# Reading the moving operand of fp32r products from two halves of its 512 columns

## The reference

```python
def first_block(x, ...):
    for layer in range(2):
        h = rms_norm(x, norm_g[layer, 0]) * (1.0 + scale) + shift
        y = nsa_mixer(h, ...) if layer % 2 == 0 else hgrn2_mixer(h, ...)
        x = x + gate * y
        h = rms_norm(x, norm_g[layer, 1]) * (1.0 + scale) + shift
        x = x + gate * hier_moe(h, ...)     # 16 experts, top 2: (silu(x @ w1) * (x @ w3)) @ w2

def second_block(x, ...):
    for l in range(2):
        x = x + 0.5 * swiglu(rmsnorm(x, ffn1_norm[l]), gate, up, down)   # 1024 -> 2752 -> 1024
        h = rmsnorm(x, mix_norm[l])
        p_a, p_b, p_c = _split(h @ w_in[l], (A_IN, B_IN, C_IN))
        o_a, o_b, o_c = rwkv7_mixer(...), dsa_mixer(...), retention_mixer(...)
        x = x + concatenate([o_a, o_b, o_c]) @ w_out[l]
        x = x + 0.5 * swiglu(rmsnorm(x, ffn2_norm[l]), gate, up, down)
    return rmsnorm(x, final_norm)
```

## Time and profile before

| | us |
|---|---|
| three runs, median | 4058.69 |
| three runs, lowest and highest | 4055.40, 4058.89 |
| the profiled execution's own time | 4054.44 |
| its span, first to last instruction | 4052.6 |
| PE busy in the span | 3887.6 (96%) |
| DVE busy, ACT busy | 2531.8 (62%), 1961.2 (48%) |
| chain of work that ended last, on PE | 80% |

### The profile page before, as it was taken

How to read it: one execution, slowest core, us unless ns; L and a number is a source line. 1 busy time by engine, 2 the same in 40 slices (tenths; PEclk the granted TensorE clock), 3 DMA queues, 4 the chain that set the end, 5 groups by cost and what they waited for, 6 DMA issues and landing times.

```text
span 4052.6 us, 59941 instructions
## 1 busy us (share of the span) xinstructions
PE 3887.6 (96%) x25080; PEld 3073.2 (76%) x25080; DVE 2531.8 (62%) x4297; ACT 1961.2 (48%) x3260; POOL 240.5 (6%) x213
## 2 busy tenths in 40 slices
PE   7999999999989999989999989999999999899998
PEld 5855788877867888868878667888788887578886
DVE  4288589985275899954456855544544469655445
ACT  3366588884364888842234434322423344343222
POOL 0033100000021000010000000000000000000000
PEclk9999999999999999999999999999999999899999
DMA  5464399982202999932222101222222221012221
GB/s 234 185 231 186 139 426 416 415 338 104 86 21 87 402 418 414 370 121 104 94 87 90 38 24 45 102 88 94 94 104 104 85 98 47 3 43 104 86 101 68
DMA packets 62566, 637.83 MB, mean 157 GB/s; under 512 B 6567, under 2 KB 6823, under 8 KB 27480
## 3 DMA queue, kind: packets, MB, share of 16 engines
q1 hardware_dynamic: 47032, 578.42, 36.3%
q0 software_dynamic: 8640, 31.46, 2.1%
q10 hardware_dynamic: 6624, 24.12, 1.5%
HBM read 603.52 MB, written 35.69 MB: 158 GB/s over the span
## 4 chain that ended last, share of the span: by engine, by line
PE 80%; DVE 12%; ACT 5%; issue 2%; DMA 1%; POOL 0%; DVEq 0%; POOLq 0%; SPq 0%; ACTq 0%
PE ps L366 13%; PE ps L370 13%; PE ps L371 13%; PE ps L1567 4%; PE ps L1569 4%; PE ps L1568 4%; DVE wbuf_r L347 3%; PE ps L1589 2%; PE ps L1588 2%; PE ps L1587 2%; DVE arena L3332 1%; DVE arena L3330 1%; PE ps L622 1%; PE ps L415 1%; PE ps L416 1%
## 5 line engine op out<-in xcount | busy, mean ns | idle before, releaser
L370 PE MATMUL ps<-arena_r,wbuf_r 128*128 128x512 f32 x2688 | 1047.5, 390 | 0.0
L347 DVE TENSOR_TENSOR wbuf_r<-slot,wbuf_r 128x512 fp32r<-128x512 f32 (+2 forms) x824 | 587.0, 723 | 652.6 <-ACT wbuf_r L337 651.1
L337 ACT ACTIVATE wbuf_r<-slot 128x512 fp32r<-128x512 f32 (+2 forms) x824 | 498.9, 613 | 623.3 <-PE ps L371 532.2
L366 PE MATMUL ps<-hT_r,wbuf_r 128*128 128x512 f32 x2016 | 794.7, 394 | 5.4 <-DVE arena_r L771 4.4
L371 PE MATMUL ps<-hT_r,wbuf_r 128*128 128x512 f32 x2016 | 786.1, 390 | 0.0
L370 PEld LDWEIGHTS ps<-arena_r,wbuf_r 128*128 128x128 f32 x2688 | 505.7, 188 | 104.7 <-issue 2.6
L366 PEld LDWEIGHTS ps<-hT_r,wbuf_r 128*128 128x128 f32 x2016 | 379.3, 188 | 95.3 <-issue 5.8
L371 PEld LDWEIGHTS ps<-hT_r,wbuf_r 128*128 128x128 f32 x2016 | 379.3, 188 | 80.0
L366 PE MATMUL ps<-arena_r,wbuf_r 128*128 128x512 f32 x704 | 277.3, 394 | 0.9 <-DVE arena_r L2780 0.9
L371 PE MATMUL ps<-arena_r,wbuf_r 128*128 128x512 f32 x672 | 261.4, 389 | 0.0
L1435 DVE TENSOR_TENSOR arena_r<-arena,arena_r 128x1024 fp32r<-128x1024 f32 x164 | 195.9, 1220 | 45.6 <-ACT arena_r L1428 45.2
(11 more groups left out here) (582 smaller groups left out, 7011.8 us busy)
## 6 DMA issues: line engine op xcount, KB each, us to landing
arena<-in_moe SPq DMA_DIRECT2D x82, 2048.0 KB, 10.6
slot<-in_moe SPq DMA_DIRECT2D x56, 2048.0 KB, 10.4
slot<-in_gu SPq DMA_DIRECT2D x40, 2048.0 KB, 7.7
slot<-in_ada SPq DMA_DIRECT2D x20, 2048.0 KB, 8.0
slot<-in_down SPq DMA_DIRECT2D x16, 2048.0 KB, 7.8
slot<-in_win SPq DMA_DIRECT2D x12, 2048.0 KB, 7.7
yrow<-arena ACTq DMA_DIRECT2D x46, 512.0 KB, 10.8
slot<-in_hgrn SPq DMA_DIRECT2D x8, 2048.0 KB, 7.9
```

The costliest lines, as they stand in the source:

```text
L337: a.activation(hi[:, 0:w], src[:, off:off + w], ACT.Copy).then_inc(*act.mark(c.name, "hi", i))
L347: v.tensor_tensor(lo[:, 0:w], src[:, off:off + w], hi[:, 0:w].bitcast(F32), ALU.subtract) \
L366: p.matmul(bank, hi[:, cs], rh[:, k, :], start=k == 0, stop=False, skip_group_check=True)
L370: p.matmul(bank, hi[:, cs], rl[:, k, :], start=False, stop=False, skip_group_check=True)
```

## The change

A helper `by_halves` gives a view of 512 columns in which positions 0, 1, 2, 3 are columns 0, 256, 1, 257 and so on: the first dimension of the access steps by 256 columns and has two elements, the second steps by one column and has 256. The moving operand of the products named above is read through this view. For the result to stand in PSUM in its usual order, the data have to lie in SBUF with the even columns in the first half and the odd ones in the second:

- weights that move are laid out so by the host (`_halved`): the experts' weights, the columns for `tok3_pe` of width 512, the scan's span matrix;
- activation tiles that move are written through the same view, by ACT (hi) and DVE (lo, which also reads the hi tile through it): the input norms of the four feed-forward stages, the gated hidden tiles, and the split outputs of the mixers.

The input projections of the mixers stay as they were (`cols=in_order`), since their tokens also serve as stationary operand; so do `tok3_pe` of width 264 and all plain f32 products. No instruction, wait, transfer or buffer is added, removed or moved: on each engine the rows stand in the same order with the same waits, and differ only in the shape of an access (an ACT write of 128x512 is 128x256x2 after the change).

```diff
+def by_halves(x):
+    return x.rearrange("p (a b) -> p b a", a=2)
+
+def in_order(x):
+    return x
...
-                    p.matmul(bank, hi[:, cs], rh[:, k, :], start=k == 0, stop=False, skip_group_check=True)
+                    p.matmul(bank, hi[:, cs], cols(rh[:, k, :]), start=k == 0, stop=False, skip_group_check=True)
...
+                hi_cols, lo_cols = (by_halves(x) if width == 512 else x for x in (hi, lo))
...
-                    p.matmul(o, rh[:, k, cs], hi, start=k == 0, stop=False, skip_group_check=True)
+                    p.matmul(o, rh[:, k, cs], hi_cols, start=k == 0, stop=False, skip_group_check=True)
...
-            a.activation(m.gh[:, f, :], m.sg[f % 4], ACT.Copy).then_inc(*act.mark(n, "g hi", part, f))
+            a.activation(by_halves(m.gh[:, f, :]), m.sg[f % 4], ACT.Copy).then_inc(*act.mark(n, "g hi", part, f))
...
-                    v.tensor_tensor(m.gl[:, f, :], sg, m.gh[:, f, :].bitcast(F32), ALU.subtract) \
+                    v.tensor_tensor(by_halves(m.gl[:, f, :]), sg, by_halves(m.gh[:, f, :].bitcast(F32)), ALU.subtract) \
...
-                            p.matmul(bank, xh[:, ks], hi[:, cs], start=k == 0, stop=False, skip_group_check=True)
+                            p.matmul(bank, xh[:, ks], by_halves(hi[:, cs]), start=k == 0, stop=False, skip_group_check=True)
...
+def _halved(w):
+    return np.ascontiguousarray(w.reshape(*w.shape[:-1], -1, 256, 2).swapaxes(-1, -2)).reshape(w.shape)
...
-    out["moe"] = np.concatenate([m1, m3, m2], axis=1)
+    out["moe"] = _halved(np.concatenate([m1, m3, m2], axis=1))
```

More of the change, by code:

```diff
@@ L348, in cut_lo, with lin3_pe @@
                 .then_inc(*dve.mark(c.name, "lo", i))
[L350 removed]
+        def lin3_pe(p, c, ps, pieces, name, count, rh, rl, end, kt=8, ready=None, first=0, stacked=False, cols=by_halves):
             for i in range(first, first + count):
@@ L374, in lin3_pe, with two3_pe @@
                 pe.also(*name, i)
-        def two3_pe(p, c, ps, pieces, name, tiles, rh, rl, end, by, ready):
+        def two3_pe(p, c, ps, pieces, name, tiles, rh, rl, end, by, ready, cols=by_halves):
             bank = [ps.take((*name, i), end(i)) for i in tiles]
```

94 lines of the change are left out of this document (49 added, 45 removed).

## The result

The changed kernel took 3999.95 us (median of 4 runs, 3998.07 to 4007.14) beside 4057.05 us for the kernel before on the same chip: a ratio of 0.9868, 95% interval 0.9849 to 0.9887. By the medians it is 57 us faster (1.4%), by the ratio 1.3%. The forecast was 121 us.

The account below looks back on a forecast made before the run. PE was taken as the bound nearly everywhere; feed-forward 74 + experts 35 + `tok3_pe` 5 + outputs 7 = 121 us off 4054.4 gave 3933, or 3937 for a median, with a range of 3905 to 4066.

Parts of the forecast that it names:

- part (221): All altered products: only the overrun growing with columns goes, 5.7 ns each, 62 us in all, 3998 us; chance 0.20.
- nothing (227): All altered products: pace unchanged, the overrun lies elsewhere, writes cost 0 to 8 us, 4058 to 4066 us; chance 0.13.
- slower (428): All altered products: alternating fetch takes two ticks a column, 2190 us lost, near 6250 us or in between; chance 0.22.
- the f32 row: Eight f32 products in the earlier trace: 428 ns each, halved 214 for 512 columns, so the overrun lies in the operand fetch.
- the 74 forecast: Feed-forward stages: 6016 products x 12.2 ns give 73 us saved, plus 1 us from products in `two3_pe`.
- 26 for 35: Expert stages: 3312 products x 12.2 ns give 40 us, of which 35 were taken as saved.
- 5 us off for DMA: Expert stages: DMA falls 0.3 to 0.7 us behind a block, partly hidden by slack, so 35 of 40 us are taken.
- The forecast's own sign for the DMA: Expert stages: if ACT begins to wait for DMA, the 35 us saved were too many.
- 0 to 2: Alternate writes by ACT and DVE: 14 uncovered input norm tiles x 0.13 to 0.7 us, 2 to 10 us; 0 to 2 taken.
- The gated tiles have the 70 us as cover: Feed-forward stages: ACT waits 70 us for the gated tile before writing g hi, which hides slower gated writes.
- the line through both widths: Products of 264 and 512 columns: fit of 6.4 ns plus 0.430 ns a column, splitting the 13 ns overrun.
- L512, L2745 and L2800 within 0.13 us: Norm and gated tile writes in the feed-forward: times expected to stay within 0.13 us of 0.75, 0.63 and 0.69 us.

Follow-up runs that it names:

- reads: Changed kernel with every activation tile written in order, all altered products still reading by halves: 3952.87 us, ratio 0.9749 to the kernel before.
- outs: Kernel before with alternate writes only in the output tiles of attention, hgrn and the two mixers: 4072.72 us beside 4050.48, ratio 1.0055.
- writes: Kernel before with only the alternate activation writes, everywhere the change has them, products reading in order: 4104.62 us, ratio 1.012.
- patterns: Code of reads, with single 512-column products each read in its own order (pairs apart, steps, parts in turn): 216 to 460 ns a product, whole time 4557 us.

## Why the forecast was wrong

**The mechanism, right.** The pace of an altered product fell, the projections beside it stayed at 227, and every other rival fell with that: part (221), nothing (227), slower (428). Nothing but the order of the moving columns differs between 216 and 227 ns, so most of the overrun was in the fetch of the moving operand, as the f32 row had suggested.

**The size of one product, near.** 216 ns and not 214.5, so 10.7 ns saved and not 12.2. The Trainium skill's "TensorE: Matmul & The Clock Gate", section "Wait — 56ns, not 53.3ns?", had 215.7, and the trace agrees. The f32 records of the earlier trace rows start 429 ns apart in the median, 2.3 ns over their two ticks a column, and the new pace is 2.7 ns over one tick a column: half of an f32 record holds only half of what each record has of its own.

**The reads, 102 of 121.** By stages, kernel before against `reads`: feed-forward stretches 345.1 to 329.5 three times and 345.1 to 328.8 once, 63 us for the 74 forecast. Experts 12.9 and 13.2, 26 for 35. `tok3_pe` 1.1 + 3.4, 4.5 for 5. Outputs 2.3 + 1.1 + 4.4 + 1.9, 10 for 7. Together 103. Of the 18 missing, 11 are in the feed-forward, where the pace alone explains 9 (6016 x 1.5 ns), and 9 in the experts, where it explains 5, less 3 gained in the outputs. That gain is partly luck: 192 products 10.7 ns faster are 2 us, and the last output got 4.4, with a clock of 1.00 where the kernel before had 0.94.

**The experts, a discount too small and for a wrong reason.** 3312 products x 10.7 ns are 35 us, of which 26 came. The forecast took 5 us off for DMA, 9 were lost, and a reading of the profile could have gone on blaming the DMA: landings grew from 10.6 to 15.8 us, the engines' DMA share stayed at 1.01, and 7.34 MB at 427 GB/s are 17.2 us, exactly a block. But half the fetch changed nothing. The forecast's own sign for the DMA, ACT waiting for it, did not appear either. The 92.5 us of DVE in 100 stood in the forecast beside it, "become 97%", and no price was put on them; a piece that DVE finishes 0.46 us late once a block was what ended last.

**The step that failed: the writes.** The forecast took "0 to 2" us and put 10 at the far end; measured 50. Two faults stand in that line. First the price. It was taken from a DVE row with one operand every 64 bytes, 31 columns, 259 ns against 251, and in that row it is a source that is read so; a scattered destination stood nowhere in the trace. The measured price, 0.43 to 0.49 us a tile, lies between the forecast's two ends (0.13 and 0.7). Thirty-one columns in 251 ns, beside 512 in 693, cannot show a price for each column well either. Second, and heavier, the count. It asked which altered tile PE waits for, and found 14. With the measured price these give 6 to 7 us, so the price alone does not explain 50. Three things were left out. The 32 output tiles were not counted at all: PE waits for 13 of them in `outs`, which took 22 us more. The untouched cuts of the weights stand in the same queues behind the norm tiles: PE's waits for them grew by 13 us in `writes`. And the granted clock stood lower: by the estimate above 17 us of the 50, 12 of them already in the 22. "The gated tiles have the 70 us as cover" held for most of them, but not for the last one of a stage: PE waited 4.3 us for it in the four stages, where it had waited 0.9.

**Small slips in the working.** A block of 72 x 226.7 + 12 x 112 ns is 17.7 us and not 17.8. Of the 13 ns over one tick a column the line through both widths gives 6.9 to the columns and 6.4 to the product; the text has them the other way round, and its rival takes 5.7 because it sets out from 214.5 and not from 213.3. The range's lower end, 3905, is some 9 us below 4058.7 - 145. None of this changes the outcome.

**What would have told.** The forecast said what would show the writes wrong, L512, L2745 and L2800 within 0.13 us; their rows in the changed kernel did, 0.4 to 0.5 us longer. The range, 3905 to 4066, held the time. It was the likeliest value that was 63 us off. That the time, 3999.95, meets the 3998 of the rival "only part of the overrun goes" is chance: that rival wanted products 221 ns apart and next to no cost in the writes, and neither came.

**The rule on lines.** Beside the rival of 6250 us stood the Trainium skill's "SBUF — State Buffer", table of specifications, which wants at least two accesses to a line of 16 bytes for full bandwidth. As a forecast for alternate reads it was wrong: one access in a row to each line ran fastest of all, 216 ns. The price that the rival had, two ticks a column, exists, 451 ns for a step of 2, though that step does touch each line twice in a row. That a line is fetched anew, as the third theory of `patterns` had it, and every price here are not in that table. For writes the rule agrees with the rows: two and two 674 ns, one and one 1142. The measurement decides: for TensorE's reads the rule sorts the table above if it is taken for every other read, and not for reads as they follow each other.

## What to carry to other kernels

A permutation of columns has to be paid somewhere, and the prices lie far apart: none in the step of a bank that VectorE reads anyway (692 ns either way), none on the host, 135 to 260 ns a tile for a stepped source in SBUF, 430 to 490 for a destination that alternates. Ask first which operation takes it for nothing. And a longer operation on a feeding engine is charged three times: to TensorE where it needs that tile at once, to everything that is queued behind it, and, by the estimate here, through a lower granted clock where TensorE waits more. So count the queue, and not only the tiles that TensorE waits for.

## What the hardware showed beyond this

- Reading a moving operand in order is not its fastest way: 227 ns for 512 fp32r columns, against 216 when two places at least 16 bytes apart are read in turn. The 4096 products of pairs 16 and 64 apart were as fast as those 1 KB apart, so alternating between two neighbouring groups of four columns (216 ns too) would do.
- An alternate destination takes 1118 to 1142 ns for 633 on ACT and 1095 to 1126 for 693 on DVE (which reads one source in the same order), at every distance tried from 16 bytes to 1 KB, and 636 and 693 within 16 bytes.
- The granted clock was lower in stretches where PE waited more: 0.70 for 0.84 in the first feed-forward start and 0.89 for 0.97 in the output of the second block's first mixer, where PE was busy for 93% of the time instead of 97. It is not the same in each execution. In the profiled one of the changed kernel the attention stretch took 251.6 us at a clock of 0.93; in `writes` and `outs`, with the same writes there, 243.1 at 0.97. So some 8 us of its 4007 seem to be no work of the change, which fits with its median of 4000.
